# Mixture-of-experts stage in four column groups: 20 steps of 4 x 32 slots with fp32 weights as they land

## The reference, cut to what matters

```python
g_idx = argmax(t @ w_group + b_group)                 # one of 4 groups
top_v, top_i = lax.top_k(e_sel, 2)                    # two of the 4 experts in it
combine = one_hot(g_idx) * within                     # (tokens, 16), two weights in each row
hg = jnp.einsum('td,edf->tef', t, w_e_gate)           # 16 x (1024, 256)
hu = jnp.einsum('td,edf->tef', t, w_e_up)             # 16 x (1024, 256)
act = jax.nn.silu(hg) * hu * combine[:, :, None]
out = jnp.einsum('tef,efd->td', act, w_e_down)        # 16 x (256, 1024)
```

## Time and profile before

| | us |
|---|---|
| median of three runs | 1387.39 |
| profiled execution | 1388.23 |
| its span in the trace | 1386.4 |
| barrier into the expert stage passed | 1010.3 |
| first gate/up matmul | 1023.60 |
| last down matmul starts | 1326.96 |
| barrier out of the expert stage passed | about 1331.1 |

### The profile page before, as it was taken

The page is one execution under the profiler, slowest core; times in us unless marked ns, Lnnn a source line. Parts: engine busy times, 40 slices in busy tenths (PEclk is TensorE's granted clock), DMA queues, the critical chain, the costliest instruction groups (busy, mean ns, idle before and its releaser), DMA issues.

```text
span 1386.4 us, 25433 instructions
## 1 busy us (share of the span) xinstructions
PE 1283.3 (93%) x9198; PEld 1112.6 (80%) x9198; DVE 994.3 (72%) x1500; ACT 739.0 (53%) x1323; POOL 130.8 (9%) x95
## 2 busy tenths in 40 slices
PE   4899999999999999999999987999389999999966
PEld 3798999999999999999999974877278887888832
DVE  2533457577585875858758567699869998999948
ACT  1344344454454544544544545422348998998825
POOL 1433200000000000000000000000011111111042
PEclk9699999999999999999999998999669999999988
DMA  9787443223342333423333343463187989555776
GB/s 325 245 274 250 131 121 102 79 83 92 91 117 69 86 100 90 117 59 88 103 94 102 97 131 106 144 214 137 76 300 252 357 308 372 197 193 181 282 254 200
DMA packets 210855, 229.41 MB, mean 165 GB/s; under 512 B 17942, under 2 KB 184666, under 8 KB 210619
## 3 DMA queue, kind: packets, MB, share of 16 engines
q1 hardware_dynamic: 195499, 173.33, 40.0%
q10 hardware_dynamic: 8280, 29.51, 5.5%
q0 software_dynamic: 6976, 25.23, 5.5%
HBM read 173.00 MB, written 46.79 MB: 159 GB/s over the span
## 4 chain that ended last, share of the span: by engine, by line
PE 73%; DVE 12%; ACT 4%; DMA 3%; issue 3%; SPq 3%; POOL 1%; ACTq 0%; DVEq 0%; POOLq 0%
PE AB L998 11%; PE AB L1002 11%; PE AB L999 11%; PE S L923 6%; PE S L925 6%; PE S L924 6%; PE S L1098 4%; ACT F L1506 3%; PE T L1124 2%; DMA F<-in_b_ada 2%; PE OB L923 2%; PE OB L924 1%; PE OB L925 1%; SPq L629 1%; ACT R L1506 1%
## 5 line engine op out<-in xcount | busy, mean ns | idle before, releaser
L1506 ACT ACTIVATE R<-F 128x1024 fp32r<-128x1024 f32 (+4 forms) x306 | 292.6, 1003 | 76.2 <-DVE F L2090 41.6
L998 PE MATMUL AB<-R 128*128 128x344 f32 x960 | 315.7, 333 | 1.2 <-ACT F L1506 1.2
L999 PE MATMUL AB<-R 128*128 128x344 f32 x960 | 304.2, 321 | 0.0
L923 PE MATMUL S<-R 128*128 128x512 f32 x480 | 192.3, 401 | 1.9 <-ACT F L1506 1.6
L925 PE MATMUL S<-R 128*128 128x512 f32 x480 | 188.1, 392 | 0.0
L924 PE MATMUL S<-R 128*128 128x512 f32 x480 | 187.9, 391 | 0.0
L998 PEld LDWEIGHTS AB<-R 128*128 128x128 f32 x960 | 181.4, 189 | 4.8 <-issue 4.6
L999 PEld LDWEIGHTS AB<-R 128*128 128x128 f32 x960 | 181.7, 189 | 1.7 <-issue 1.7
L1002 PE MATMUL AB<-R 128*128 128x344 f32 x960 | 171.6, 320 | 0.0
L1506 ACT ACTIVATE F<-AB 128x344 f32<-128x344 f32 (+3 forms) x129 | 59.1, 460 | 210.0 <-PE AB L1002 194.3
L1002 PEld LDWEIGHTS AB<-R 128*128 128x128 f32 x960 | 155.6, 188 | 0.0
(11 more groups left out here) (296 smaller groups left out, 2261.5 us busy)
## 6 DMA issues: line engine op xcount, KB each, us to landing
F<-in_w_ada SPq DMA_DIRECT2D x24, 1024.0 KB
F<-in_w_in SPq DMA_DIRECT2D x44, 512.0 KB, 4.2
F<-in_w_e_gate SPq DMA_DIRECT2D x16, 1024.0 KB, 7.2
F<-in_w_e_up SPq DMA_DIRECT2D x16, 1024.0 KB, 11.0
F<-in_w_e_down SPq DMA_DIRECT2D x16, 1024.0 KB, 8.8
y_d<-F ACTq DMA_DIRECT2D x32, 512.0 KB, 7.8
out<-F SPq DMA_DIRECT2D x24, 512.0 KB, 4.0
F<-F SPq DMA_DIRECT2D x192, 43.0 KB, 1.9
```

Of the source, the lines that this page charges most:

```text
L923: mm(out, w[0], m[1], start=start, stop=False)
L998: mm(bank[:, 0:PIECE], whl[b][0][:, k, :], x[1][:, k, :], start=(k == 0), stop=False)
L999: mm(bank[:, 0:PIECE], whl[b][0][:, k, :], x[0][:, k, :], start=False, stop=False)
L1506: return nc.scalar.activation(out, in_, func, **kw)
```

## The change

1. Slots of an expert are rounded up to 32, not 128 (`LANE = 32`). That is 80 subtiles of 32 slots, 20 steps of four. Column group j takes subtiles 20j to 20j + 19 in order, one a step. So in a step the four quarters of a 128-row tile can belong to four experts. With the counts above 72 subtiles hold tokens, and the experts of the four groups over the 20 steps are

```diff
-SLOT_TILES = (2 * T + NE * (P - 1)) // P
+LANE = 32
+EXPERT_LANES = P // LANE
+STEPS = (2 * T + NE * (LANE - 1)) // LANE // EXPERT_LANES
...
+            sp.wait_ge(wout_ready, NT + 1)
+            for q in range(2):
+                load_gate_up(0, 0, q)
+            load_down(0, 0)
...
+            sp.wait_ge(te_ready, 1)
+            first = [None] + [expert(j, 0) for j in range(1, EXPERT_LANES)]
+            for q in range(2):
+                for j in range(1, EXPERT_LANES):
+                    load_gate_up(first[j], j, q)
+            for j in range(1, EXPERT_LANES):
+                load_down(first[j], j)
             stage_end(sp, 1)
...
+                with sp.If(of[0] + of[1] + of[2] + of[3] != before[0] + before[1] + before[2] + before[3]):
+                    for q in range(2):
+                        sp.wait_ge(gu_used, 2 * n - 1 + q)
+                        for j in range(EXPERT_LANES):
+                            next_gate_up(of[j], before[j], j, q)
...
+        def gate_up(n):
+            b = n % 2
+            if n >= 2:
                 pe.wait_ge(av_done, n - 1)
             for q in range(2):
+                pe.wait_ge(xT_done_, 2 * n + q + 1)
+                for j in range(EXPERT_LANES):
+                    gu_landed[j][q].wait(pe, 32 * (n + 1))
                 for k in range(4 * q, 4 * q + 4):
-                    last = mm3(Sb[b], [x[:, k, :] for x in hg[b]], [w[:, k, :] for w in gu[b]], start=(k == 0), stop=(k == KC - 1))
+                    for j in range(EXPERT_LANES):
+                        rows = slice(LANE * j, LANE * j + LANE)
+                        last = mm(Sb[b][rows, :], xT[b][:, k, rows], gu[j][:, k, :], start=(k == 0), stop=(k == KC - 1), skip_group_check=True)
+                last.then_inc(gu_used, 1)
...
+        for n in range(STEPS):
+            silu4(n)
+            if n:
+                before, of = of, [expert(j, n) for j in range(EXPERT_LANES)]
+                rows_out(n - 1)
+                with act.If(of[0] + of[1] + of[2] + of[3] != before[0] + before[1] + before[2] + before[3]):
+                    for j in range(EXPERT_LANES):
+                        next_down(of[j], before[j], j)
```

More of the change, by code:

```diff
@@ L78, in constants @@
     put("row", p[None, :])
-    put("start", P * np.arange(SLOT_TILES)[None, :])
+    put("start", LANE * np.arange(STEPS)[None, :])
+    put("first", LANE * p[:, None])
     valid = np.ones((P, NT + 1))
@@ L1435, in turn_act, with down @@
             last.then_inc(avT_ready, 1)
-        def down(n, b, later):
-            pe.wait_ge(avT_hi, n + 1)
-            pe.wait_ge(avT_lo, n + 1)
-            pe.wait_ge(dn_hi, n * 2 + 2)
-            pe.wait_ge(dn_lo, n * 2 + 2)
-            if later:
+        def down(n):
+            pe.wait_ge(avT_done, n + 1)
+            for j in range(EXPERT_LANES):
+                dn_landed[j].wait(pe, 16 * (n + 1))
+            if n:
                 pe.wait_ge(y_copied, n)
@@ L1445, in down @@
                 for c in range(2):
-                    last = mm3(Sb[2 + q], [a[:, c, :] for a in aT], [w[:, c, 512 * q:512 * q + 512] for w in dn[b]],
-                               start=(c == 0), stop=(c == 1))
+                    for j in range(EXPERT_LANES):
+                        rows = slice(LANE * j, LANE * j + LANE)
+                        last = mm(Sb[2 + q][rows, :], aT[:, c, rows], dn[j][:, c, 512 * q:512 * q + 512],
+                                  start=(c == 0), stop=(c == 1), skip_group_check=True)
@@ L1448, in down @@
             last.then_inc(dn_used, 1)
-        def tile4(n, b, landed, before, more=True):
-            if more:
-                turn_rows(n + 1, 1 - b, landed, True)
-            if before >= 1:
-                turn_act(n - 1, before >= 2)
-            gate_up(n, b, before >= 2)
-            if before >= 1:
-                down(n - 1, 1 - b, before >= 2)
-        pe.wait_ge(ws_ready, 1)
-        for c in range(2):
-            for t in range(NT + 1):
-                n, rows = 9 * c + t, P if t < NT else NS
-                last = mm(PB[:, 0:SLOT_TILES], row_hot[0:rows, n, :].bitcast(F32), tile_w[0:rows, n, :], start=(n == 0), stop=(n == 17))
@@ L1477, in _ @@
+        turn_act(STEPS - 1)
+        down(STEPS - 1)
         stage_end(pe, 2)
@@ new lines, in act4 @@
+        def act4(n):
+            dve.wait_ge(avT_ready, n + 1)
+            if n:
+                dve.wait_ge(dn_used, n)
+            nc.vector.tensor_copy(aT, PB[:, 0:FF].rearrange("p (a b) -> p a b", a=2)).then_inc(avT_done, 1)
+        rows4(0)
+        for n in range(STEPS):
+            if n + 1 < STEPS:
+                rows4(n + 1)
+            if n:
+                act4(n - 1)
+            else:
+                dve.wait_ge(ws_ready, 2)
+                mark(nc.vector.tensor_copy(wslot[:, :], PB[:, 0:STEPS]), ws_copied, 1)
+            gated(n)
@@ L2718, in _ @@
         pool.wait_ge(slots_done, 1)
-        gather(0, 0, 0, False)
+        gather(0)
         stage_end(pool, 1)
-        for n in range(1, SLOT_TILES):
-            gather(n, n % 2, n // 2 + (n % 2) * HALF, n >= 2)
+        for n in range(1, STEPS):
+            gather(n)
         stage_end(pool, 2)
```

393 lines of the change are left out of this document (153 added, 240 removed).

## The result

The changed kernel takes 1403.78 us (median of 4 runs, 1402.03 to 1405.6), the kernel before 1387.39 (1387.28 to 1391.54; a fourth execution beside it, of 2509.93 us, was a slow one and is left out): ratio 1.0114, 95% interval 1.0097 to 1.0131. It is slower by about 1.1%, and the forecast was 1380.

What follows compares the result with a forecast made beforehand. The expert stage was taken to be bounded by TensorE. Gaining 47.6 us without stalls and losing 40 us to stalls left it 7.6 us earlier, so 1380 us, range 1362 to 1406.

Steps and rivals of the forecast that it cites:

- Part 1: One expert-stage step on TensorE: sets of four 0.43 us apart, 12.0 us a step, bounds 11.7 to 12.3.
- Rival C: TensorE's 512-column sets of four take 0.59 us each, adding 78 us: 1458; chance 0.04.
- Part 2: Way into the expert stage: barrier at 1019 to 1020, gate/up at 1034 instead of 1023.60 after the second gather.
- Part 3: Expert stage without stalls: barrier out at 1283.5 against 1331.1, 47.6 us gained.
- Part 4: TensorE's stalls for weight loads at changes of expert: together 40 us, barrier out at 1323.5.
- single change: Steps changing one expert: no gate/up stall, down at most 1.2 us late, 0.6 x 10 = 6 us taken.
- Step 3: Step changing two experts: second halves of gate/up 3 us, down 5, together 8.
- Step 19: Last step, changing three experts: gate/up halves 4.5 and 5.4 us late, down 13, half clock +3.4; sum 26.
- Rival A: Down loads land in 8.8 us, so ten single changes cost 28 us instead of 6: 1404; chance 0.29.

Runs made afterwards that it cites:

- no_loads: The changed kernel with steps 1 to 19 loading no weights and computing with the first ones: 1331.58 us (one run).
- small_gather: The changed kernel with the gathers of steps 2 to 19 bringing 8 rows instead of 128: 1384.39 us (8 runs).
- down_first: The changed kernel with ScalarE issuing down loads ahead of the result rows and their store: 1378.62 us, ratio to before 0.9947.
- best1: down_first plus step 1's gather ahead of the barrier into the expert stage and x1 reloads in steps without a change: 1370.03 us, ratio to before 0.9863.

## Why the prediction was wrong

**Part 1, a step: right.** 12.0 forecast, 11.68 measured, just under the lower bound of 11.7. Sets of four run 0.43 us apart: the 16 sets of gate/up take 6.89 us, from 1136.48 to the first `down` at 1143.37. Rival C's 0.59, 78 us more, is excluded. The rule of the Trainium skill that stood behind it ("TensorE: Matmul & The Clock Gate", section "Measured speedup vs the span model") gives the length of one pack; taken as the distance of packs in a row, as the prediction took it for this rival, these rows disagree with it. Over 19 steps the miss is -6.1 us.

**Part 2, the way in: mechanism right, size off.** Barrier at 1019.3 (forecast 1019 to 1020), the second gather behind it, TensorE waiting for it. It landed some 7 us after its issue, not 10 to 13, so gate/up began at 1029.31 instead of 1034. Step 1 starts 4.7 us earlier than forecast.

**Part 3: right.** 47.6 forecast without stalls. no_loads is 55.5 below the kernel before: 47.6 + 6.1 + 4.7 from the two misses above, - 1.6 for the cold start of step 1 and - 3.6 at the last `down`, and 3.2 from its earlier step 1 make 56.4.

**Part 4, the stalls: this failed, and it decided.** The step is "With 7.2 it lands 9.6 after the last down, wanted after 8.4 ... I take 0.6 x 10 = 6." The 2.4 us to the issue and the 8.4 to the need were right (step 7: last `down` over at about 1146.9, issue at 1149.42, wanted at 1159.54 - 4.30 = 1155.24). The landing was not: 8.0 us on the mean of the ten (6.3 to 10.1), from issue to the start of `down`. I had the best case of before for a load beside the store alone; small_gather shows that the gather is there as well, and it is most of the difference. 2.4 + 8.0 - 8.4 = 2.0 us of wait each, 20.5 in all. Two of the ten then ran `down` partly at half clock (5.23 and 5.34), which my sum gave no single change: 3.3 more. The rest is some 0.2 us at each restart. Together 25.9 from the step lengths, against 6.

Step 3 was to cost 8: second halves 3, down 5. It costs 17.5: waits of 1.64, 4.70 and 5.31, and half clock behind two of them (6.13 and 6.51 instead of 3.64), which the sum had put at nothing here too. Step 19 was to cost 26 and costs 27.7.

The sum by these sizes: 1323.5 - 4.7 - 6.1 + 19.9 (single changes) + 9.5 (step 3) + 1.7 (step 19) + 1.6 (a cold start of step 1, which I had left out) = 1345.4, and the barrier is at 1345.2. Rival A had the mechanism of the single changes, 28 against 25.9. That it had the time too, 1404, is partly luck: its landing of 8.8 was too long, it gave steps 3 and 19 only 2 us more where they took 11.2, and it shared the 10.8 us that Parts 1 and 2 had too many. What I held against it, that a queue of its own would free the down load, was half true: 8.8 became 7.7, but the time from issue to need was only 6.0 (8.4 - 2.4).

That the changed kernel lost to the one before by the order of issue, and not by the column groups, is shown by down_first: one moved call turns 1.0114 into 0.9947. It gives back 25 us of the 72.7. What steps 3 and 19 cost, where two and three experts change at once, mostly stays: 39.9 us in its trace, 45.2 in the changed kernel's. Whether a second buffer for each group would end those waits is open; no run tried it.

## What to carry to other kernels

When weights stop being a side matter, work out for each load the slack between its earliest issue and its need, and hold it against the landing beside everything that starts at the same event, not against the best landing on record; here a slack of 6.0 us against a landing of 7.7 was a loss at every change. Put the load that someone waits for ahead of the one that nobody waits for in its queue: 25 us for one moved call. And before filling a wait to keep the clock, or moving bytes to another stage, ask whether the next wait or that stage ends with a transfer: here they did, and neither paid.

## What the runs showed of the hardware that I had not expected

- TensorE's granted clock is half behind many waits for loads, and the work there takes longer: 32 instructions of `down` take 3.64 us at 2.4 GHz and 5.2 to 6.5 us when they follow waits of 3.10 to 12.69 us in the changed kernel, where waits of up to 2.22 us left them at 3.64. Elsewhere a 1.90 us wait was followed by 5.34 (no_loads) and one of 3.02 by 3.64 (step 3 of best1), so the wait's length alone doesn't decide. With products that nobody reads in the wait, the product behind it took 3.64.
- Of a 1 MB load and a 0.5 MB store on one queue, the one that is issued second lands late. With their order turned round the load's median landing went from 7.7 to 6.0 us, the store's from 2.9 to 6.5.
- The order in a queue costs even with no load in it: ScalarE's copy of result rows, the store's issue and its branches stood ahead of the signal for the last `down` and held it 1.90 us in no_loads.
